# Scaled tokens get memory of their own, and the sixth expert slot waits for the stores alone

## The reference

```
x = x + merged @ w_o[i]
x = x + hierarchical_moe(rmsnorm(x, g_ffn[i]), w_router_group[i], ..., w_exp_gate[i], w_exp_up[i], w_exp_down[i])
x = x + (p[i] @ w_ple[i]) * sigmoid(rmsnorm(x, g_ple[i]) @ w_ple_gate[i])
```

## Time and profile before

| | |
|---|---|
| median of 3 runs | 2428.04 us (2426.86 to 2429.57) |
| the profiled execution | 2430.51 us, its span 2428.7 us |
| busy in the span | PE 2286.0 us (94%), PEld 1698.3 (70%), DVE 1001.9 (41%), ACT 586.9 (24%), POOL 411.5 (17%) |
| granted TensorE clock, mean | 0.982 |
| expert weights, SP's queue | 192 transfers of 1024 KB in the two layers |
| DMA in the 40 slices of the span | 418 to 423 GB/s in six slices, in the two expert stages; 20 to 137 in most others |

### The profile page before, as it was taken

One profiled execution on the slowest core, in us unless ns is written; L12 is line 12 of the kernel. 1 busy time (PEld: TensorE's weight loads), 2 busy tenths in 40 slices (PEclk: granted clock), 3 DMA queues, 4 the chain that ended last, 5 costly groups with the idle time before them and its releaser, 6 DMA issues. The chain is left out here.

```text
span 2428.7 us, 29699 instructions
## 1 busy us (share of the span) xinstructions
PE 2286.0 (94%) x11860; PEld 1698.3 (70%) x11860; DVE 1001.9 (41%) x1763; ACT 586.9 (24%) x1210; POOL 411.5 (17%) x407
## 2 busy tenths in 40 slices
PE   7989999997889989999998888999989999999998
PEld 6667788654457767788754446877768887888887
DVE  5544533511145454643521126445653435332234
ACT  3533401311133342410311115223540002000012
POOL 2011111122211101111122121111101121111211
PEclk9999999999999999999999999999999999999999
DMA  5114536799961202233899982322213332333322
GB/s 162 51 47 107 130 111 251 320 421 423 418 234 56 70 20 79 66 96 137 330 420 422 422 328 89 91 84 81 83 42 96 94 115 78 96 97 100 98 96 71
DMA packets 291930, 396.57 MB, mean 163 GB/s; under 512 B 32590, under 2 KB 232014, under 8 KB 274378
## 3 DMA queue, kind: packets, MB, share of 16 engines
q1 hardware_dynamic: 274880, 366.27, 42.1%
q0 software_dynamic: 11328, 16.81, 1.9%
q10 hardware_dynamic: 5578, 11.51, 1.8%
HBM read 388.98 MB, written 30.15 MB: 173 GB/s over the span
## 5 line engine op out<-in xcount | busy, mean ns | idle before, releaser
L146 PE MATMUL banks<-h_split,w_high 128*128 128x512 f32 x2624 | 825.6, 396 | 2.8 <-PEq L3325 1.7
L146 PEld LDWEIGHTS banks<-h_split,w_high 128*128 128x128 f32 x2624 | 481.0, 188 | 104.3 <-issue 8.2
L198 DVE TENSOR_TENSOR w_low<-w_raw,w_high 128x1024 fp32r<-128x1024 f32 (+1 forms) x264 | 317.1, 1201 | 503.5 <-POOL w_high L187 503.5
L187 POOL CAST w_high<-w_raw 128x1024 fp32r<-128x1024 f32 (+1 forms) x264 | 277.7, 1053 | 1455.5 <-PE banks L146 1325.5
L146 PE MATMUL banks<-h_split,w_low 128*128 128x512 f32 x1312 | 512.1, 390 | 0.0
L146 PEld LDWEIGHTS banks<-h_split,w_low 128*128 128x128 f32 x1312 | 246.3, 188 | 52.6
L146 PE MATMUL banks<-w_high,op_split 128*128 128x512 f32 x736 | 228.5, 390 | 1.6 <-DVE mg_part L1358 1.1
L2091 PE MATMUL banks<-expert_ring,ex_xsT 128*64 128x256 f32 x1408 | 172.7, 401 | 32.9 <-DMA expert_ring<-in_w_exp_up 32.9
L2091 PEld LDWEIGHTS banks<-expert_ring,ex_xsT 128*64 128x64 f32 x1408 | 102.4, 144 | 90.9 <-DMA expert_ring<-in_w_exp_up 36.1
L146 PEld LDWEIGHTS banks<-w_high,op_split 128*128 128x128 f32 x736 | 138.2, 188 | 32.1 <-DVE mg_part L1358 2.4
L146 PE MATMUL banks<-w_low,op_split 128*128 128x512 f32 x368 | 143.2, 389 | 0.0
(11 more groups left out here) (448 smaller groups left out, 2740.1 us busy)
## 6 DMA issues: line engine op xcount, KB each, us to landing
w_raw<-in_w_in SPq DMA_DIRECT2D x142, 512.0 KB, 3.9
expert_ring<-in_w_exp_gate SPq DMA_DIRECT2D x42, 1024.0 KB, 20.6
expert_ring<-in_w_exp_up SPq DMA_DIRECT2D x42, 1024.0 KB, 23.8
expert_ring<-in_w_exp_down SPq DMA_DIRECT2D x42, 1024.0 KB, 23.6
region<-in_w_exp_gate SPq DMA_DIRECT2D x22, 1024.0 KB, 19.8
region<-in_w_exp_up SPq DMA_DIRECT2D x22, 1024.0 KB, 23.7
region<-in_w_exp_down SPq DMA_DIRECT2D x22, 1024.0 KB, 23.6
w_raw<-in_w_gu SPq DMA_DIRECT2D x44, 512.0 KB, 4.0
```

What stands on the lines that cost most here:

```text
L146: last = nc.tensor.matmul(out, left, right, start=(start and n == 0), stop=(stop and n == 2), skip_group_check=True)
L187: self.nc.gpsimd.tensor_copy(self.high[:, i % self.SPLIT, 0:n], self.raw[:, i % self.RAW, 0:n]).then_inc(self.high_ready, 1)
L198: self.nc.vector.tensor_tensor(self.low[:, i % self.SPLIT, 0:n], self.raw[:, i % self.RAW, 0:n], self.high[:, i % self.SPLIT, 0:n].bitcast ...
```

## The change

Four things change. The scaled tokens `norm.xn` move to memory at `e.turned_at`, where the buffers `ex_xsT` and those behind it lie, which nobody uses before the first gather has landed. ACT scales and stores tiles 0 and 1 before the eviction of the logits, DVE scales tiles 2 and 3 in front of its wait for the logits, and ACT stores them after the eviction. The matrix `select` moves to the second gather buffer (`e.select_at`), for which DVE waits until POOL has cleared it. `first_token` is taken ahead of two steps of DVE's chain, and 13 in place of 18 unread products follow. SP issues the sixth slot when the stores have landed, without waiting for the first gather.

```diff
-        norm = Norm(k, ctx, "ffn", None, (0, 1, 2, 3, 4, 5), k.spare_tiles, True, (r.ss, r.gain))
+        scaled = nc.alloc_sbuf_tensor_at("rt_scaled" + k.layer, [P, NT, D], F32, offset=e.turned_at)[:]
+        norm = Norm(k, ctx, "ffn", None, (0, 1, 2, 3, 4, 5), scaled, True, (r.ss, r.gain))
...
-        select = nc.alloc_sbuf_tensor_at("rt_select" + k.layer, [P, NT, FIRST_PAIR, LANES], F32R, offset=e.second_at)
+        select = nc.alloc_sbuf_tensor_at("rt_select" + k.layer, [P, NT, FIRST_PAIR, LANES], F32R, offset=e.select_at)
...
             sp.wait_ge(norm.stored, 16 * NT)
-            sp.wait_ge(e.gathered[0], 16)
             expert_loads.issue(sp, 10)
...
-            unread(k, 3, 18)
+            unread(k, 3, 13)
...
             norm.following_root(act)
+            act.wait_ge(norm.rstd_ready, 1)
+            for t in (0, 1):
+                nc.scalar.activation(norm.xn[:, t, :], k.x[:, t, :], ACT.Copy, scale=norm.ss[:, t:t + 1]).then_inc(norm.xn_act, 1)
+            for t in (0, 1):
+                act.wait_ge(norm.xn_act, t + 1)
+                nc.scalar.dma_start(xn_rows[t * P:(t + 1) * P, :], norm.xn[:, t, :]).then_inc(norm.stored, 16)
             act.wait_ge(logits_done, 1)
             nc.scalar.activation(lgT, k.ps[:, 6, 0:S // 2], ACT.Copy).then_inc(logits_out, 1)
-            act.wait_ge(norm.rstd_ready, 1)
-            for t in range(NT):
-                nc.scalar.activation(norm.xn[:, t, :], k.x[:, t, :], ACT.Copy, scale=norm.ss[:, t:t + 1]).then_inc(norm.xn_act, 1)
-                if t:
-                    act.wait_ge(norm.xn_act, t)
-                    nc.scalar.dma_start(xn_rows[(t - 1) * P:t * P, :], norm.xn[:, t - 1, :]).then_inc(norm.stored, 16)
-            act.wait_ge(norm.xn_act, NT)
-            nc.scalar.dma_start(xn_rows[(NT - 1) * P:, :], norm.xn[:, NT - 1, :]).then_inc(norm.stored, 16)
+            for t in (2, 3):
+                act.wait_ge(norm.xn_dve, t - 1)
+                nc.scalar.dma_start(xn_rows[t * P:(t + 1) * P, :], norm.xn[:, t, :]).then_inc(norm.stored, 16)
...
+            for t in (2, 3):
+                V.tensor_scalar(norm.xn[:, t, :], k.x[:, t, :], norm.ss[:, t:t + 1], None, ALU.mult).then_inc(norm.xn_dve, 1)
             dve.wait_ge(logits_turned, 1)
...
+            dve.wait_ge(cleared, GATHERS)
             V.tensor_tensor(select[:], lane_next[:].unsqueeze(1).unsqueeze(1).to_broadcast([P, NT, FIRST_PAIR, LANES]),
                             next_rank[:].unsqueeze(3).to_broadcast([P, NT, FIRST_PAIR, LANES]), ALU.is_equal).then_inc(select_ready, 1)
             link(V.tensor_tensor(beyond[:], neg_counts.unsqueeze(1).to_broadcast([P, FULL, NE]),
                                  neg_base[:].unsqueeze(2).to_broadcast([P, FULL, NE]), ALU.is_lt))
+            dve.wait_ge(first_tabled, 1)
+            V.tensor_scalar(first_token[:], k.ps[:, 7, P:P + 1], 2.0 * S, None, ALU.add).then_inc(first_ready, 1)
             link(V.tensor_reduce(out=spills[:], in_=beyond[:].rearrange("p f e -> p e f"), axis=AX.X, op=ALU.add),
                  V.tensor_tensor(slotv[:], tiled(base[:, 0:NE], NE), neg_ranks, ALU.subtract))
-            dve.wait_ge(first_tabled, 1)
-            V.tensor_scalar(first_token[:], k.ps[:, 7, P:P + 1], 2.0 * S, None, ALU.add).then_inc(first_ready, 1)
...
-        second_at = nc.sbuf_base + 4 * DC * P
+        turned_at = nc.sbuf_base
...
-        e.second_at = second_at
+        e.turned_at, e.select_at = turned_at, turned_at - 4 * D
```

More of the change, by code:

```diff
@@ L73, in __init__ @@
         self.layer = ""
-        offset = self.aligned(ctx, "region")
+        offset = self.region_at = self.aligned(ctx, "region")
         self.region = sb("region", [P, 3 * NT * D])
```

## The result

The changed kernel takes 2439.50 us (median of 6 runs, 2436.94 to 2442.88); the kernel before, run beside it, 2429.52 (2426.86 to 2432.45). The ratio is 1.0043 [1.0033, 1.0054]: 10 us slower, where 1.3 us faster was forecast. The profiled span went from 2428.7 to 2440.0 us.

The account below looks back on a forecast made before the run. Expert weights streaming over full DMA engines bound the stage. Per layer, 3.7 us less a 2.2 us delay gained 1.5, or -0.2 with half clock; one layer of each gave 1.3 us, 2426.7 us, range 2420.8 to 2431.5.

Parts of the forecast that it names:

- The landing of the gather: First gather beside the sixth slot's load: lands 7.0 us after issue (bounds 4.4 and 8.6), weight products 2.2 us later.
- part 4: Expert stage's start: the first gather shares the DMA with the sixth slot; 2.2 us delay, plus 1.7 us half clock once.
- rival B: First weight products: gather comes last, half clock in both layers; delay 5.5 us, 3.6 us slower, 2431.6; chance 0.13.
- The half clock: Expert 0's first products after TensorE's pause: 1.2 GHz level costs 1.7 us, taken in one of two layers.
- The gain of an earlier sixth slot: First refill finds the DMA free, landing after 4.7 us instead of 8.8; 3.7 us per layer after gathers' 0.4.
- the eviction of the logits was not held up: ACT's early scalings and stores fit its idle time before the eviction, still at 438.59; cost 0, bounds 0 to 0.3.
- The gap in the loads ahead of the refill: Sign in the DMA windows: a short gap before the first refill's gate, which lands about 5 us after its issue.
- Rival A: First gather hardly slowed beside the load: delay 0.45 to 0.9 us, gain 5.6 to 6.5, 2421.5 to 2422.4; chance 0.31.
- the two rules of the Trainium skill: DMA engines: queues take turns by packet, costing the gather 1.2 us; or its completion signal waits behind the load's bytes.

Follow-up runs that it names:

- e2: The kernel before with only SP's wait for the first gather taken out ahead of the sixth slot's load; 2437.93 us, ratio 1.0038.
- e13: The kernel before, but SP issues the sixth slot once POOL has issued the first gather, not when it has landed; 2427.69 us, ratio 0.9988.
- e12: The changed kernel with the sixth slot issued once POOL has issued the first gather, and 20 covering products; 2429.51 us, ratio 0.9996.
- e9: The changed kernel with the sixth slot issued once POOL has issued the first gather, and 29 covering products; 2431.19 us, ratio 1.0001.

## Why the prediction was wrong

The sum forecast a gain of 1.3 us over the two layers; the stages lost 9.5. The difference of 10.8 has three terms, read from the starts in the timelines above, of one profile each. The first two are measured by themselves; the third is what they leave of the stages.

- **The landing of the gather (part 4), 3.3 us.** I took 7.0 us, from the second gathers' 7.6 and 6.3; it took 8.0 and 8.2. The transposes came 3.2 and 4.5 us late, 7.7 in all, where 2 x 2.2 = 4.4 was forecast. The nearest row was right in kind, and rival B's 8.6 was nearer in size. Its objection, that the first gather has none ahead in its queue, was wrong in what it left out: it has the first 1.6 MB of the load ahead, in another queue.
- **The half clock (part 4), 4.7 us.** This is the largest term. I priced it at 1.7 us, in one layer of two. It came in both, and from the transposes to the first refill it cost 2.8 and 3.6 us, 6.4 in all. In the first layer that is 0.8 on the transposes (1.94 for 1.14), 0.7 between them and the weight products, and 1.3 on these (4.94 for 3.67); in the second 0.9, 0.2 and 2.4. My 1.7 counted the weight products alone. "I take it in one of the two" had no ground either: the prediction's own pause, 4.05 us (450.6 to 454.65), was of the kind of which it had counted 3 of 3 at half clock. The real pauses were 6.2 and 7.2 us, also because 13 covering products took 3.22 us and not 4.3 (the 18 of before ran at 0.33 us each, these at 0.25; the row of 18 was taken in part at the lower clock, 0.79 at 446 to 448, and the 18 of e2 took 4.35 us).
- **The gain of an earlier sixth slot, 2.9 us.** Forecast 3.7 for each layer; what the profiles leave for it is the refill's delay less the stage's, 6.0 - 3.5 = 2.5 and 8.1 - 6.1 = 2.0. The step that failed is that I took the first layer's landing of the first refill, 8.8 us, for both. In the second layer of the kernel before it was 7.0, where the sixth slot had been issued 1 us sooner (12.8 after the eviction for 13.8):

```profile
region<-in_w_exp_gate SPq DMA_DIRECT2D x1, 1024.0 KB, 7.0
```

So 7.0 - 4.7 - 0.4 = 1.9 was to be had there, and 2.0 came. That a refill into free DMA engines lands after 4.7 us, no view shows, since nothing waits for that landing. The first layer's 2.5 for 3.7 is not accounted for; the stage's end follows the first refill only to a us or so: e2, with its refills at 25.8 and 28.1 (changed kernel 25.6 and 27.7), has its last weight products at 246.8 and 248.3 (245.6 and 249.6). e13 tries this term alone: its sixth slot is issued 3.1 and 2.2 us earlier than before, its refills at 19.9 and 19.8 as before, and it gains 2.2 us by the medians, where the prediction's term is 7.4.

3.3 + 4.7 + 2.9 = 10.9, with rounding the 10.8.

What was right: the eviction of the logits was not held up (ACT still idles 0.85 us before it, DVE 0.55 before its step); the stores landed inside the bounds, the sixth slot issued 8.03 us after the eviction, which is 446.6 on the clock of before (bounds 444.2 to 447.9, taken 445); the first layer's gather was issued at 447.5 on that clock, as forecast. The second layer's came 0.3 us later than before and not earlier: in both layers it now waited for the stores. The gap in the loads ahead of the refill was to be short and was 7.5 and 9 us. What came was rival B, a late gather and half clock in both layers, which had a chance of 0.13 and a delay of 5.5 us; the delays were 6.0 and 8.1. Its 2431.6 was too low because of the pieces of half clock and the second layer's smaller gain. Rival A (gather hardly slowed) fell, though it had 0.31.

Beside this stand the two rules of the Trainium skill that the prediction weighed ("DMA: Bandwidth & Descriptors", section "Queues, rings and completion order"). Turns between the queues, packet by packet, are not what the trace shows while the gather waits: q1 has 118 packets at 452 to 454 and q0 none (whether the gather's packets stood in the DMA engines' queues by then, no view shows). From 454 to 456, with 80 packets and 70, it looks like turns. That a completion lands only after every earlier write of its engine agrees with e12, where a load issued later does not hold the gather's signal (4.6 and 3.4 us), and does not conflict with the changed kernel's 8.0 and 8.2. But there the packets themselves were late, which that rule does not say, and the gather landed with its last packets (449.54 + 8.0 = 457.5), while the load's moved until 459.5; so the prediction's reading, that the signal is held behind the load's bytes, is not what the runs show.

## What to carry to other kernels

A small transfer on the critical path that is issued behind a bulk load can wait for much of it even from another queue (here for 1.6 to 1.7 MB); issue it first and let the bulk follow at once, on a signal of its issue and not of its landing. Price a wait that leaves TensorE idle with everything that then runs at the lower clock up to the next step that others wait for, not with the one group of products that a row shows. And where a stage repeats, read each term in every repetition before it is doubled.

## What the runs showed of the hardware

- Pauses of TensorE ahead of the transposes, over the 28 of all these profiles (two for each of the fourteen kernels): eleven of up to 0.84 us, and behind all of them the first weight products took 3.67 us; ten of 2.95 us and over, and behind all of them 4.94 to 6.54. Of the seven between, 1.07 to 1.96 us, three ended at 3.67 (1.70, 1.93, 1.96) and four at 5.07 to 5.36 (1.07, 1.48, 1.63, 1.67): there the length of the pause did not tell. The clock fell without a pause of that kind too: in the kernel before it was 0.79 at 446 to 448 and 0.50 at 448 to 450, with TensorE busy for the whole 2.00 us of both.
- A gather of POOL issued 0.8 to 0.9 us behind a 3 MB load of SP's queue moved its first packet 4.5 us after its issue, and under 2 us after it where it was issued ahead of the load (e9).
- In the first layer the stores of 512 KB land 3.0 us after their issue in the kernel before (median of four) and 6.4 in the changed one, where they were issued while the third slot's load was still flowing. Of the time by which they were issued earlier nothing was left: the sixth slot, which waits for them, went 8.0 us after the eviction, and 7.8 in e2 with the stores of before.
